# Seven block products for the gate projections of a hybrid encoder block, and half of the merged tensor through DRAM

## The chip, the cores and the metric

The kernel runs on all 8 cores of one Trainium2 chip, one batch element of 2048 tokens on each core, with the same weights everywhere and no exchange between cores. The metric is device time of the slowest core in microseconds, from one execution to the next the median of the runs.

## The reference, cut to what matters

Every token is normalised and goes through one wide input projection. Two branches (a gated convolution, `y_c`, and a diagonal state-space scan, `y_s`) are built from the first 5120 columns; the last 4096 columns are the logits of two sigmoid gates, and the branches meet under these gates:

```python
xn = _rmsnorm(h, norm_g)
proj = jnp.einsum("bld,de->ble", xn, w_in)
v_c, g_c, z_c, u_s, z_s, gl_c, gl_s = _split_columns(proj)
...
gate_c = jax.nn.sigmoid(gl_c + b_gate[:D_MODEL])
gate_s = jax.nn.sigmoid(gl_s + b_gate[D_MODEL:])
merged = (gate_c * jnp.einsum("ble,ed->bld", y_c, w_conv)
          + gate_s * jnp.einsum("ble,ed->bld", y_s, w_ssm))
h = h + jnp.einsum("bld,de->ble", merged, w_out)
out = _rmsnorm(h, final_g)
```

D_MODEL is 2048, `y_c` and `y_s` have 1024 channels each. 16 meta tokens are put in front of the 2048 and dropped at the end. The gate logits are a product of 4096 columns with 2048 inputs for each token, the largest single product of the block.

## The kernel before, in words

Channels lie on the 128 partitions, tokens run along the free dimension. Matmuls take bf16 operands, 128 x 128 weights against 512 tokens, into one of 8 PSUM banks. On-chip memory is cut by hand into regions: XM (the normalised tokens, 16 blocks of 128 channels), CY (working space, later the two branches `CBv` and `YSv`), WS (weights), ST (everything short-lived) and SM (small parameters). Tokens are held in eight chunks `j` of 258 (time modulo 8; two of the 258 belong to the meta tokens), so a block `n` of 512 tokens is two chunks read in two runs of 256; `rt(n)` is that view.

The stages follow one another: normalisation with the first projections, the scan and the convolution, the z projections (written to DRAM in `z_scr` and read back through the slots `zr`), layer norm and the GLU of the scan branch (lines 1096 to 1155), then the stage that the change rewrites (lines 1180 to 1205), then the output projection with its normalisation (lines 1208 to 1349).

The rewritten stage runs over two halves `h` of the tokens and 16 tiles `j` of 128 output channels; the text calls one pair (h, j) a unit. A unit loads three weight tiles through the POOL queue (`gload`, eight rotating slots in WS): the two gates' 2048 x 128 weights and the branch tile, 1024 x 128 for each branch. For each of its two blocks of 512 tokens it runs two gate projections of 16 matmuls, a sigmoid of each on ScalarE (`gst`, fp32), two branch projections of 8 matmuls, a multiply of each with its gate on VectorE (`stt`) and an addition of the two into the merged tensor (`tt`). A unit so has 64 gate and 32 branch matmuls. The merged tensor of half 0 is kept in ST, that of half 1 in XM over the tokens of half 0 (`MGv`).

The output stage then takes 16 blocks of 128 tokens in the order of `blocks`, multiplies each with w_out (64 matmuls, four banks of 512 columns), adds x, which `o_load` fetches on the SP queue, and normalises. w_out replaces the branches in CY and the tokens of half 1 in XM as these are freed.

The order of the instructions is not written by hand. `Sched` (line 73) is a list scheduler that runs while the program is built: each operation carries an engine, an estimated duration, its dependences and a priority (`prio`, lower first); the scheduler steps through a model time, and each free engine takes the ready operation with the lowest priority number, then the earliest in program order. The resulting order of each engine and each DMA queue is fixed, and `resolve` adds semaphore waits for the dependences. A buffer (`Buf`) is an interval of a region, so that reuse of space makes a wait as well. Main matmuls have priority 40 (`P_MAIN`), evictions 3.

Of the kernel before, what the change touches and what calls it, by code (L numbers as in the profile page):

```python
# [22 lines left out]
NC = L // T  # L23
# [322 lines left out]
def build():  # L346
    nc = bass.Bass("TRN2", target_bir_lowering=False)
    Buf.registry = {}
    S = Sched()
# [10 lines left out]
    w_main = din("w_main", [72, 128, 2048])  # L360
    w_br = din("w_br", [16, 128, 2048])
# [5 lines left out]
    def scratch(name, shape):  # L367
        return nc.dram_tensor(name, list(shape), BF16).ap()
# [5 lines left out]
    c_scr = scratch("c_scr", [8, 8, 128, NR])  # L374
    z_scr = scratch("z_scr", [16, 128, SEQ])
    k_scr = scratch("k_scr", [8, 8, 16, 240])

    es = ExitStack()
    with es:
# [25 lines left out]
        def tile(region, lo, nbytes, dt=BF16):  # L405
            return view(region, lo, nbytes, dt), Buf((region, lo, lo + nbytes))


        def act(out_, in_, func, bias=0.0, scale=1.0, accum=None, n=512, reads=(), writes=(), **kw):
            kw["tab"] = {AF.Sqrt: "sqrt", AF.Exp: "exp", AF.Ln: "exp", AF.Sin: "silu", AF.Tanh: "silu", AF.Silu: "silu",  # L410
                         AF.Sigmoid: "sigmoid", AF.Gelu_apprx_tanh: "gelu"}.get(func)
            if accum is None:
                f = lambda e: e.activation(out=out_, in_=in_, func=func, bias=bias, scale=scale)  # L413
            else:
                f = lambda e: e.activation(out=out_, in_=in_, func=func, bias=bias, scale=scale, accum_out=accum)
            return S.op("act", f, 0.22 + n / 1200.0, reads, writes, **kw)

        def tt(out_, in0, in1, op, n=512, rate=0.96, reads=(), writes=(), eng="dve", **kw):
            d = 0.15 + n / (rate * 1000.0) if eng == "dve" else 0.3 + n * 2.2e-3
            return S.op(eng, lambda e: e.tensor_tensor(out=out_, in0=in0, in1=in1, op=op), d, reads, writes, **kw)  # L420
# [628 lines left out]
        def rt(n):  # L1049

            return lambda k: XMv[:, k, 2 * n * NC:(2 * n + 2) * NC].rearrange("p (j c) -> p j c", j=2)[:, :, 2:NC]

        def xrt(n):
            return xb_of(2 * n * NC, (2 * n + 2) * NC)
# [43 lines left out]
        zr = [tile("ST", 36864 + i * 2048, 2048) for i in range(3)]  # L1098
        zr_n = [0]

        zr += [tile("ST", 6144 + i * 2048, 2048) for i in range(8)]

        def z_load(mm, h, prio):
            i = zr_n[0] % 3 if mm > 7 else 3 + mm
            zr_n[0] += 1
            dma("sp", [(zr[i][0], z_scr[mm][:, h * 1024:(h + 1) * 1024])], f"zr{i}", 128 * 2048,
                (zscB[mm][2 * h], zscB[mm][2 * h + 1]), (zr[i][1],), prio=prio)
            return zr[i]
# [30 lines left out]
        for n in range(4):  # L1139
# [11 lines left out]
            if n % 2:  # L1151
# [8 lines left out]
        MGB_ = [[[Buf((("ST", j * 2048 + q * 1024, j * 2048 + q * 1024 + 1024) if h == 0 else  # L1160
                       ("XM", j * L * 2 + q * 1024, j * L * 2 + q * 1024 + 1024))) for q in range(2)] for j in range(16)]
                for h in range(2)]
        gst = [tile("ST", 32768 + i * 2048, 2048, F32) for i in range(4)]
        all_n = [0]

        def any_bank():
            b = all_n[0] % 8
            all_n[0] += 1
            return b

        gn = 0
        g_slot = [0]
        marks = []

        def gload(src_ap):
            s_ = g_slot[0] % 8
            g_slot[0] += 1
            return wload(s_, src_ap, 33, after=(zm,) if 6 <= g_slot[0] <= 8 else ())

        for h in range(2):  # L1180
            for j in range(16):
                gw = [gload(w_main[40 + 2 * j])[:2], gload(w_main[41 + 2 * j])[:2]]
                b3, brB, _ = gload(w_br[j])
                for n in (2 * h, 2 * h + 1):
                    q = n % 2
                    dst = MGv[h][:, j, q * 512:q * 512 + 512]
                    gs = []
                    for br_ in range(2):
                        bk = any_bank()
                        proj(gw[br_][0], gw[br_][1], 0, rt(n), 512, xrt(n), bk)  # L1190
                        g_, gB = gst[gn % 4]
                        gn += 1
                        bc = PAR["bgate"][:, 16 * br_ + j:16 * br_ + j + 1]
                        act(g_, ps[bk], AF.Sigmoid, bias=bc, reads=(psB[bk], psmB), writes=(gB,), prio=3)
                        gs.append((g_, gB))
                    for br_, (sv, sB) in enumerate(((CBv, CBq), (YSv, YSq))):
                        bk = any_bank()
                        proj(b3[:, br_ * 8:br_ * 8 + 8, :], brB, 0, lambda k: sv[:, k, n * 512:(n + 1) * 512], 512,
                             [sB[k][n] for k in range(8)], bk, nk=8, halves=1)
                        g_, gB = gs[br_]  # L1200

                        stt(g_, ps[bk], 1.0 - 0.5 * br_, g_, ALU.mult, ALU.mult, reads=(psB[bk], gB), writes=(gB,), prio=3)
                    mk = tt(dst, gs[0][0], gs[1][0], ALU.add, reads=(gs[0][1], gs[1][1]), writes=(MGB_[h][j][q],), prio=3)
                    if h:
                        marks.append(mk)


        CYk = CY[:, :].rearrange("p (k t) -> p k t", k=16)
# [33 lines left out]
            fst.append((v_, b_))  # L1242
        xp = x.rearrange("(c j) d -> j c d", j=8)
        op_ = out.rearrange("(c j) d -> j c d", j=8)
        blocks = [(j, hf) for j in range(8) for hf in range(2)]

        def o_load(i):
            j, hf = blocks[i]
            v_, b_ = ht[i % 8]
            dma("sp", [(v_, xp[j, 128 * hf:128 * hf + 128, :].rearrange("c (n t) -> c n t", n=4))], f"ht{i % 8}",  # L1250
                128 * 8192, (), (b_,), prio=6)
# [79 lines left out]
        FIRST = 8  # L1331
        for i in range(8):
            o_load(i)
        for i in range(FIRST):
            for n in range(2):
                o_mm(i, n)
# [136 lines left out]
```

How the kernel before makes its waits and increments, by code:

```python
    def emit(self, name, eng):  # L335
        for waits, o, sig in self.prog[name]:
            for sem, v in waits:
                eng.wait_ge(sem, v)
            last = len(o.fns) - 1
            for i, fn in enumerate(o.fns):
                ins = fn(eng)
                if o.dsrc is not None or i == last:
                    ins.then_inc(sig[0], sig[1])
# [1016 lines left out]
                @block.sync  # L1360
                def _(e):
                    S.emit("sp", e)
                    for src, v in last.values():
                        e.wait_ge(src.sem, v)
```

## Time and profile before

| | |
|---|---|
| median of 3 runs | 1683.8 us |
| lowest and highest | 1683.55 and 1696.59 us |
| profiled execution, span of its slowest core | 1678.5 us |
| spans of the 8 cores in it | 1665.3 to 1678.5 us |
| PE, VectorE, ScalarE, POOL busy | 1631.0, 706.7, 554.6, 106.9 us |
| rewritten stage | 784.06 to 1447.10 us of the span |
| output stage | from 1447.10 us |

The span is from the first to the last instruction on a core. The profiled execution has no time of its own on the page beside its span; the runs were timed apart from it, and their times contain what lies around the span. PE is the matrix engine, PEld its weight loads, DVE the VectorE, ACT the ScalarE. Matmuls are pipelined, and their ends are modelled, so that one takes 380 ns in a row although the next starts long before; the distance from start to start is read from counts over a stretch.

### The profile page before, as it was taken

To read this page: it belongs to the slowest core of one execution; us is meant where nothing else is said; L and a number is where in the kernel's file an instruction comes from. 1 tells how busy PE (TensorE), PEld (TensorE's weight loads), DVE (VectorE), ACT (ScalarE), POOL (GpSimd) and SP (SyncE) were. 2 spreads that over 40 slices of the span, in tenths; PEclk is the share of its full clock that TensorE was granted. 3 is DMA by queue.
4 is the path that set the end of the run, shared out by engine and by line. 5 is a ranking of instruction groups with operands and counts; after the bars stand their busy time and mean duration, and the time that the engine had idled before them with its cause. 6 is when DMAs were issued, how large, how long until landed. Compare 5 with 4: busy or idle time off the path is not lost.

```text
span 1678.5 us, 25748 instructions; the slowest of 8 cores (1665.3 to 1678.5 us)
## 1 busy us (share of the span) xinstructions
PE 1631.0 (97%) x9426; PEld 928.3 (55%) x9512; DVE 706.7 (42%) x1262; ACT 554.6 (33%) x954; POOL 106.9 (6%) x206
## 2 busy tenths in 40 slices
PE   7999989998999999999999999999999999999997
PEld 6888868887855444444444444444444444444443
DVE  3799158786777110578111111111111221225433
ACT  4564346454455169554111111111111111122222
POOL 1000000010001000000100000000110100100000
PEclk9999999999999999999999999999999999999999
DMA  9935979889577654443644444445555553837612
GB/s 239 218 90 103 144 95 148 143 142 145 110 153 161 160 148 98 113 108 94 113 76 75 76 76 76 76 76 89 100 93 92 101 93 81 184 98 237 215 76 76
DMA packets 115163, 200.86 MB, mean 120 GB/s; under 512 B 19424, under 2 KB 68832, under 8 KB 112864
## 3 DMA queue, kind: packets, MB, share of 16 engines
q0 software_dynamic: 33792, 92.29, 35.2%
q1 hardware_dynamic: 80672, 105.35, 22.9%
q8 instruction: 78, 1.28, 0.3%
q10 hardware_dynamic: 576, 1.58, 0.3%
q14 instruction: 45, 0.37, 0.1%
HBM read 248.92 MB, written 42.53 MB: 174 GB/s over the span
## 4 chain that ended last, share of the span: by engine, by line
PE 89%; DMA 4%; DVE 2%; SPq 2%; issue 2%; ACT 1%; DVEq 0%; ACTq 0%; POOLq 0%
PE ps L446 88%; DMA WS<-w_dw 2%; SPq L458 2%; DVE CY L420 1%; DMA WS<-w_main 1%; DMA CY<-x_t 1%; DMA CY<-u_scr 1%; ACT CY L413 0%; DVE CY L431 0%; PE ps L737 0%; ACT L413 0%; DVE XM L431 0%; DVE ST L431 0%; PE ps L725 0%; DVE CY L979 0%
## 5 line engine op out<-in xcount | busy, mean ns | idle before, releaser
L446 PE MATMUL ps<-XM,WS 128*128 128x258 bf16 (+1 forms) x6144 | 1044.0, 329 | 5.9 <-DVE XM L431 2.2
L446 PEld LDWEIGHTS ps<-XM,WS 128*128 128x128 bf16 x6144 | 603.1, 98 | 409.5 <-issue 12.9
L413 ACT ACTIVATE ST<-ps,SM 128x512 f32<-128x512 f32 (+2 forms) x224 | 137.2, 626 | 622.8 <-PE ps L446 619.2
L431 DVE SCALAR_TENSOR_TENSOR ST<-ps,ST 128x512 f32<-128x512 f32 x132 | 91.3, 692 | 529.1 <-PE ps L446 529.1
L446 PE MATMUL ps<-CY,WS 128*128 128x512 bf16 x1217 | 282.3, 379 | 3.3
L446 PEld LDWEIGHTS ps<-CY,WS 128*128 128x128 bf16 x1280 | 125.1, 98 | 151.1
L420 DVE TENSOR_TENSOR CY<-CY 128x512 bf16<-128x512 f32 (+4 forms) x184 | 120.9, 658 | 28.0 <-PE ps L446 11.4
L413 ACT ACTIVATE ST<-ps 128x258 f32<-128x258 f32 (+1 forms) x136 | 65.0, 483 | 148.7 <-PE ps L446 145.2
L420 DVE TENSOR_TENSOR CY<-ps,CY 128x514 f32<-128x514 f32 (+2 forms) x97 | 66.1, 683 | 109.7 <-PE ps L446 108.8
L413 ACT ACTIVATE CY<-CY 128x514 f32<-128x514 f32 (+3 forms) x112 | 82.3, 751 | 55.9 <-DVE CY L420 30.4
L458 POOL DMA_DIRECT2D WS<-w_main x104 | 55.2, 531 | 684.9 <-PE ps L446 530.2
L420 DVE TENSOR_TENSOR ST<-ST 128x512 f32<-128x512 f32 (+3 forms) x87 | 56.0, 650 | 68.0 <-ACT ST L1090 47.2
L420 DVE TENSOR_TENSOR CY<-CY,ST 128x512 f32<-128x512 f32 (+3 forms) x115 | 64.3, 594 | 14.0 <-DMA CY<-par_b 7.0
L436 ACT CAST ST<-ps 128x258 bf16<-128x258 f32 (+1 forms) x96 | 41.9, 438 | 64.3 <-PE ps L446 58.5
L446 PE MATMUL ps<-CY 128*128 128x256 bf16 (+1 forms) x320 | 52.6, 279 | 8.6 <-DMA CY<-u_scr 5.7
L431 DVE SCALAR_TENSOR_TENSOR XM<-CY,SM,ST 128x258 bf16<-128x258 f32 x128 | 52.8, 483 | 19.2 <-ACT ST L413 19.2
L446 PE MATMUL ps<-XM 128*128 128x512 bf16 (+1 forms) x267 | 56.3, 367 | 0.3
L446 PE MATMUL ps<-CY,XM 128*128 128x512 bf16 x251 | 56.1, 379 | 0.3
L446 PE MATMUL ps<-CY,ST 128*128 128x512 bf16 x251 | 55.2, 380 | 0.3
L446 PE MATMUL ps<-XM,ST 128*128 128x512 bf16 x251 | 55.2, 380 | 0.3
L413 ACT ACT_TABLE_LOAD x35 | 44.9, 1283 | 27.0 <-PE ps L446 13.5
L446 PE MATMUL ps<-ST,WS 128*128 128x256 bf16 x320 | 41.9, 281 | 10.5 <-DMA WS<-w_dw 8.9
(82 smaller groups left out, 799.4 us busy)
## 6 DMA issues: line engine op xcount, KB each, us to landing
WS<-w_main POOLq DMA_DIRECT2D x104, 512.0 KB, 6.3
WS<-w_br POOLq DMA_DIRECT2D x32, 512.0 KB, 6.2
CY<-x_t SPq DMA_DIRECT2D x30, 516.0 KB, 17.6
WS<-w_dw POOLq DMA_DIRECT2D x32, 320.0 KB, 9.5
z_scr<-ST SPq DMA_DIRECT2D x64, 128.0 KB, 3.1
ST<-z_scr SPq DMA_DIRECT2D x32, 256.0 KB, 3.4
WS<-x SPq DMA_DIRECT2D x8, 1024.0 KB, 8.5
CY<-x SPq DMA_DIRECT2D x8, 1024.0 KB, 12.4
```

What stands on the lines that cost most here:

```text
L413: f = lambda e: e.activation(out=out_, in_=in_, func=func, bias=bias, scale=scale)
L420: return S.op(eng, lambda e: e.tensor_tensor(out=out_, in0=in0, in1=in1, op=op), d, reads, writes, **kw)
L431: return S.op("dve", lambda e: e.scalar_tensor_tensor(out=out_, in0=in0, scalar=scalar, in1=in1, op0=op0, op1=op1), 0.15 + n / 960.0, read ...
L436: return S.op("act", lambda e: e.copy(out=out_, in_=in_), 0.22 + n / 1200.0, reads, writes, **kw)
L446: return lambda e: e.matmul(a[0], a[1], a[2], start=a[3], stop=a[4])
L458: return lambda e: e.dma_start(out=o, in_=i, allow_slow_non_contiguous=True)
```

## The change

In each unit but the first of each half (j = 0), the gate logits of 256 output columns (both gates) and 1024 tokens are computed as a 2 x 2 block product by the Winograd form of Strassen's scheme. Blocks of the weights are gate (conv, ssm) by half of the 2048 inputs, blocks of the tokens are half of the inputs by block of 512 tokens. There are seven products of 8 matmuls each instead of eight. Three sums of the tokens (`T3`, `T2`, `T4`, new tiles in ST) and one in place in XM are made once per half by VectorE (`token_sums`, after the j = 0 unit), four sums of the weights in each unit. Four of the products accumulate in one bank, `ba`; ScalarE copies the bank out between them, and VectorE adds another bank to three of the copies.

ST so has no room for the merged tensor of half 0: each of its pieces goes through a small tile to DRAM (`m_scr`) and comes back into ST on the SP queue before its output blocks. The output stage takes the blocks of half 1 first. The weights go into two fixed sets instead of eight slots, `gst` has seven places instead of four, and `zr` has one place less. The load of w_out and the output stage itself are as before. A cut diff:

```diff
+    m_scr = scratch("m_scr", [16, 128, 1024])
...
-        zr += [tile("ST", 6144 + i * 2048, 2048) for i in range(8)]
+        zr += [tile("ST", 8192 + i * 2048, 2048) for i in range(7)]
 
         def z_load(mm, h, prio):
-            i = zr_n[0] % 3 if mm > 7 else 3 + mm
+            i = zr_n[0] % 3 if mm > 7 else 3 + mm % 7
...
+        mscB = [[Buf() for _ in range(2)] for _ in range(16)]
+        mst = [tile("ST", 38912 + i * 1024, 1024) for i in range(4)]
+        gst = [tile("ST", lo, 2048, F32) for lo in (22528, 24576, 26624, 28672, 16384, 18432, 20480)]
...
+        T3, T2, T4 = [view("ST", lo, 8192).rearrange("p (k t) -> p k t", k=8) for lo in (30720, 0, 8192)]
+        TB = [[Buf(("ST", lo + i * 4096, lo + i * 4096 + 4096)) for i in range(2)] for lo in (30720, 0, 8192)]
...
+        def token_sums(h):
+            n0, n1 = 2 * h, 2 * h + 1
+            t4 = lambda t, i: t[:, 4 * i:4 * i + 4, :].rearrange("p k (j c) -> p k j c", j=2)
+            kw = dict(n=2048, rate=1.92, prio=4.5)
+            for i in range(2):
+                (b11, r11), (b12, r12), (b21, r21), (b22, r22) = xq(n0, i), xq(n1, i), xq(n0, 2 + i), xq(n1, 2 + i)
+                tt(t4(T3, i), b22, b12, ALU.subtract, reads=r22 + r12, writes=(TB[0][i],), **kw)
+            for i in range(2):
+                (b11, r11), (b12, r12), (b21, r21), (b22, r22) = xq(n0, i), xq(n1, i), xq(n0, 2 + i), xq(n1, 2 + i)
+                tt(t4(T2, i), t4(T3, i), b11, ALU.add, reads=r11 + [TB[0][i]], writes=(TB[1][i],), **kw)
+            for i in range(2):
+                (b11, r11), (b12, r12), (b21, r21), (b22, r22) = xq(n0, i), xq(n1, i), xq(n0, 2 + i), xq(n1, 2 + i)
+                tt(b12, b12, b11, ALU.subtract, reads=r11 + r12, writes=r12, **kw)
+            for i in range(2):
+                (b11, r11), (b12, r12), (b21, r21), (b22, r22) = xq(n0, i), xq(n1, i), xq(n0, 2 + i), xq(n1, 2 + i)
+                tt(t4(T4, i), b21, t4(T2, i), ALU.subtract, reads=r21 + [TB[1][i]], writes=(TB[2][i],), **kw)
...
+        def product(bk, wv, wB, rhs, rB, first):
+            def mk(k):
+                return lambda e: e.matmul(ps[bk], wv[:, k, :], rhs(k), start=first and k == 0, stop=k == 7, skip_group_check=True)
+            return S.op("pe", [mk(k) for k in range(8)], 8 * 0.2157, [wB] + rB, (psB[bk],), prio=P_MAIN)
...
+        def merge(h, j, q, g0, g1):
+            (a, aB), (b, bB) = g0, g1
+            if h:
+                marks.append(tt(MGv[1][:, j, q * 512:q * 512 + 512], a, b, ALU.add, reads=(aB, bB), writes=(MGB_[1][j][q],), prio=3))
+                return
+            mt, mB = mst[(2 * j + q) % 4]
+            tt(mt, a, b, ALU.add, reads=(aB, bB), writes=(mB,), prio=3)
+            dma("sp", [(m_scr[j][:, q * 512:q * 512 + 512], mt)], f"ms{(2 * j + q) % 4}", 128 * 1024, (mB,), (mscB[j][q],), prio=5,
+                store=True)
...
-                gw = [gload(w_main[40 + 2 * j])[:2], gload(w_main[41 + 2 * j])[:2]]
-                b3, brB, _ = gload(w_br[j])
...
-                        proj(gw[br_][0], gw[br_][1], 0, rt(n), 512, xrt(n), bk)
...
+                t_ = 16 * h + j
+                (wc, ws_, b3), (wcB, wsB, brB), ((wc0B, wc1B), (ws0B, ws1B)), (s1, s2), (s1B, s2B) = gset[t_ % 2]
+                for e, src in ((0, w_main[40 + 2 * j]), (1, w_main[41 + 2 * j]), (2, w_br[j])):
+                    dma("pool", [((wc, ws_, b3)[e], src.rearrange("p (k n) -> p k n", k=16))], f"g{t_ % 2}{e}", 128 * 2048 * 4, (),
+                        ((wcB, wsB, brB)[e],), prio=33)
+                if j == 0:
+                    for q in range(2):
...
+                    token_sums(h)
+                    continue
+                kw = dict(n=1024, rate=1.92, prio=8)
+                a11, a12, a21, a22 = wc[:, 0:8, :], wc[:, 8:16, :], ws_[:, 0:8, :], ws_[:, 8:16, :]
+                tt(s1, a21, a22, ALU.add, reads=(ws0B, ws1B), writes=(s1B,), **kw)
+                tt(s2, s1, a11, ALU.subtract, reads=(s1B, wc0B), writes=(s2B,), **kw)
+                tt(a21, a11, a21, ALU.subtract, reads=(wc0B, ws0B), writes=(ws0B,), **kw)
+                ba, bb, bc = any_bank(), any_bank(), any_bank()
+                rq = lambda n, kh: [XB[jj][q] for jj in (2 * n, 2 * n + 1) for q in (2 * kh, 2 * kh + 1)]
+                xk = lambda n, kh: (lambda k: rt(n)(8 * kh + k))
+                tk = lambda t: (lambda k: t[:, k, :])
+                gc0, gc1, gs0, gs1 = gslot(), gslot(), gslot(), gslot()
+                product(ba, a11, wc0B, xk(n0, 0), rq(n0, 0), True)
+                cp("act", gc0[0], ps[ba], reads=(psB[ba],), writes=(gc0[1],), prio=2.5)
+                product(bb, a12, wc1B, xk(n0, 1), rq(n0, 1), True)
+                tt(a12, a12, s2, ALU.subtract, reads=(s2B, wc1B), writes=(wc1B,), **kw)
+                tt(gc0[0], ps[bb], gc0[0], ALU.add, reads=(psB[bb], gc0[1]), writes=(gc0[1],), prio=3)
+                gate(gc0, gc0[0], gc0[1], 0, j)
+                product(ba, s2, s2B, tk(T2), TB[1], False)
+                cp("act", gc1[0], ps[ba], reads=(psB[ba],), writes=(gc1[1],), prio=2.5)
+                product(bc, s1, s1B, xk(n1, 0), rq(n1, 0), True)
+                product(ba, a21, ws0B, tk(T3), TB[0], False)
+                cp("act", gs1[0], ps[ba], reads=(psB[ba],), writes=(gs1[1],), prio=2.5)
+                tt(gs1[0], ps[bc], gs1[0], ALU.add, reads=(psB[bc], gs1[1]), writes=(gs1[1],), prio=3)
+                gate(gs1, gs1[0], gs1[1], 1, j)
+                branch(h, j, 0, 0, gc0, b3, brB)
+                product(ba, a22, ws1B, tk(T4), TB[2], False)
+                gate(gs0, ps[ba], psB[ba], 1, j)
+                branch(h, j, 1, 1, gs1, b3, brB)
+                product(bc, a12, wc1B, xk(n1, 1), rq(n1, 1), False)
+                tt(gc1[0], ps[bc], gc1[0], ALU.add, reads=(psB[bc], gc1[1]), writes=(gc1[1],), prio=3)
+                gate(gc1, gc1[0], gc1[1], 0, j)
+                branch(h, j, 0, 1, gs0, b3, brB)
+                merge(h, j, 0, gc0, gs0)
+                branch(h, j, 1, 0, gc1, b3, brB)
+                merge(h, j, 1, gc1, gs1)
...
-        blocks = [(j, hf) for j in range(8) for hf in range(2)]
+        blocks = [(j % 8, hf) for j in range(4, 12) for hf in range(2)]
...
+        for q in range(4):
+            dma("sp", [(MG0[:, 4 * q:4 * q + 4, :], m_scr[4 * q:4 * q + 4].rearrange("k p t -> p k t"))], f"mg{q}", 128 * 8192,
+                [b for k in range(4 * q, 4 * q + 4) for b in mscB[k]], [b for k in range(4 * q, 4 * q + 4) for b in MGB_[0][k]],
+                prio=7, packets=512)
```

`branch` is the old branch projection with its multiply, `gate` the old sigmoid, `gslot` the next place of `gst`, `xq` the view of four channel blocks of one block of tokens, `gset` the two weight sets.

## Rows read from the trace of the kernel before

**Rows 1.** The page: busy time per engine, and the chain that ended last.

```profile
PE 1631.0 (97%) x9426; PEld 928.3 (55%) x9512; DVE 706.7 (42%) x1262; ACT 554.6 (33%) x954; POOL 106.9 (6%) x206
...
PE 89%; DMA 4%; DVE 2%; SPq 2%; issue 2%; ACT 1%; DVEq 0%; ACTq 0%; POOLq 0%
```

**Rows 2.** Windows: stretch, length, busy by engine (instructions), clock, DMA share, GB/s.

```profile
784.06:1447.10 663.04, 660.06 (x3017) 300.28 (x3073) 141.73 (x207) 89.92 (x130) 60.02 (x107) 1.00 0.49 86
...
300.00:400.00 100.00, 92.89 (x827) 79.75 (x825) 75.79 (x153) 50.72 (x104) 9.63 (x18) 0.96 0.91 140
...
500.00:600.00 100.00, 97.95 (x501) 49.52 (x501) 42.24 (x78) 41.31 (x74) 6.44 (x12) 0.97 0.68 160
...
700.00:800.00 100.00, 99.64 (x458) 45.25 (x463) 70.12 (x112) 45.16 (x65) 4.14 (x8) 1.00 0.40 106
```

**Rows 3.** Groups, 784 to 1447: shape, count, busy us, mean ns, idle before.

```profile
L446 PEld LDWEIGHTS ps<-XM,WS 128*128 128x128 bf16 x2048 | 200.2, 98 | 241.8
L446 PEld LDWEIGHTS ps<-CY,WS 128*128 128x128 bf16 x1024 | 100.1, 98 | 120.9
L413 ACT ACTIVATE ST<-ps,SM 128x512 f32<-128x512 f32 x128 | 88.0, 687 | 567.5 <-PE ps L446 567.5
L431 DVE SCALAR_TENSOR_TENSOR ST<-ps,ST 128x512 f32<-128x512 f32 x127 | 87.8, 692 | 514.2 <-PE ps L446 514.2
```

**Rows 4.** The chain in order of time: start, length, one link of this stretch.

```profile
980.47 10.74 PE ps L446 x49
```

**Rows 5.** Groups, 784 to 805: the z multiplies at the end of the GLU.

```profile
L420 DVE TENSOR_TENSOR CY<-CY,ST 128x1024 bf16<-128x1024 bf16 x9 | 5.8, 684 | 2.5 <-DMA ST<-z_scr 2.5
```

**Rows 6.** Timeline, three places: start, length, instruction, idle time before it.

```profile
744.77 39.66 PE L446 MATMUL ps<-CY,WS 128*128 128x512 bf16 x179
744.88 0.69 ACT L413 ACTIVATE ST<-ps,SM 128x512 bf16<-128x512 f32 x1 [0.40 <-PE ps L446]
...
780.00 0.80 ACT L413 ACTIVATE ST<-ST,SM 128x512 f32<-128x512 f32 x1
780.90 0.69 DVE L420 TENSOR_TENSOR CY<-ST 128x512 bf16<-128x512 f32 x1 [2.10 <-ACT ST L413]
...
1514.14 2.35 DVE L431 SCALAR_TENSOR_TENSOR WS<-WS,SM,ST 128x2048 f32<-128x2048 f32 x1 [0.18 <-DVE SM L440]
```

**Rows 7.** Windows around the start of the stretch (third busy column is VectorE).

```profile
780.00:790.00 10.00, 9.95 (x47) 4.55 (x47) 6.56 (x11) 4.82 (x7) 0.00 (x0) 1.00 0.20 60
790.00:800.00 10.00, 9.95 (x47) 4.49 (x46) 6.43 (x11) 1.38 (x3) 2.03 (x4) 1.00 0.01 2
800.00:810.00 10.00, 9.95 (x47) 4.54 (x47) 2.08 (x3) 1.37 (x2) 1.14 (x3) 1.00 0.99 152
```

**Rows 8.** The page: DMA issues, count, KB each, median us to landing.

```profile
WS<-w_br POOLq DMA_DIRECT2D x32, 512.0 KB, 6.2
...
ST<-z_scr SPq DMA_DIRECT2D x32, 256.0 KB, 3.4
```

**Rows 9.** Tiles: SP's last z loads and first x loads, with their starts.

```profile
L458 SPq DMA_DIRECT2D ST<-z_scr x26: 319/320/322, 703.6 to 784.9; - x26
...
L458 SPq DMA_DIRECT2D WS<-x x8: 328/340/457, 1406.1 to 1543.4; - x8
```

**Rows 10.** Windows after the stretch; the last two columns are DMA share, GB/s.

```profile
1440.00:1450.00 10.00, 9.95 (x47) 4.57 (x47) 2.08 (x3) 1.37 (x2) 2.96 (x4) 1.00 1.08 203
...
1470.00:1480.00 10.00, 9.95 (x47) 4.56 (x47) 2.08 (x3) 1.93 (x5) 0.00 (x0) 1.00 1.11 271
1480.00:1490.00 10.00, 9.95 (x47) 4.50 (x47) 2.08 (x3) 1.81 (x7) 0.00 (x0) 1.00 0.32 107
1490.00:1500.00 10.00, 10.00 (x48) 4.52 (x47) 1.93 (x3) 2.04 (x6) 0.00 (x0) 1.00 0.00 0
1500.00:1510.00 10.00, 9.95 (x47) 4.57 (x47) 1.71 (x4) 2.17 (x6) 0.00 (x0) 1.00 0.01 2
```

More of the change, by code:

```diff
@@ L1162, in build @@
                 for h in range(2)]
-        gst = [tile("ST", 32768 + i * 2048, 2048, F32) for i in range(4)]
+        mscB = [[Buf() for _ in range(2)] for _ in range(16)]
+        mst = [tile("ST", 38912 + i * 1024, 1024) for i in range(4)]
+        gst = [tile("ST", lo, 2048, F32) for lo in (22528, 24576, 26624, 28672, 16384, 18432, 20480)]
         all_n = [0]
@@ L1169, in any_bank, with gslot @@
             return b
-        gn = 0
-        g_slot = [0]
-        marks = []
[L1175 to L1178, printed above, removed]
+        gst_n = [0]
+        def gslot():
+            gst_n[0] += 1
+            return gst[(gst_n[0] - 1) % 7]
+        T3, T2, T4 = [view("ST", lo, 8192).rearrange("p (k t) -> p k t", k=8) for lo in (30720, 0, 8192)]
+        TB = [[Buf(("ST", lo + i * 4096, lo + i * 4096 + 4096)) for i in range(2)] for lo in (30720, 0, 8192)]
@@ new lines, in xq @@
+        def xq(n, q):
+            v = XMv[:, 4 * q:4 * q + 4, 2 * n * NC:(2 * n + 2) * NC].rearrange("p k (j c) -> p k j c", j=2)[:, :, :, 2:NC]
+            return v, [XB[2 * n][q], XB[2 * n + 1][q]]
+        def token_sums(h):
[14 more added lines that the diff above has]
+                tt(t4(T4, i), b21, t4(T2, i), ALU.subtract, reads=r21 + [TB[1][i]], writes=(TB[2][i],), **kw)
@@ new lines, in build @@
+        marks = []
+        gset = []
+        for i in range(2):
+            lo = 16384 * i
+            w = [tile("WS", lo + 4096 * e, 4096) for e in range(3)]
+            v = [t.rearrange("p (k n) -> p k n", k=16) for t, _ in w]
+            hb = [[Buf(("WS", lo + 4096 * e + 2048 * u_, lo + 4096 * e + 2048 * u_ + 2048)) for u_ in range(2)] for e in range(2)]
+            sums = [tile("WS", lo + 12288 + 2048 * e, 2048) for e in range(2)]
+            gset.append((v, [b for _, b in w], hb, [t.rearrange("p (k n) -> p k n", k=8) for t, _ in sums], [b for _, b in sums]))
@@ new lines, in branch, with gate @@
+        def branch(h, j, q, br_, g, b3, brB):
+            n = 2 * h + q
+            sv, sB = ((CBv, CBq), (YSv, YSq))[br_]
+            bk = any_bank()
+            proj(b3[:, br_ * 8:br_ * 8 + 8, :], brB, 0, lambda k: sv[:, k, n * 512:(n + 1) * 512], 512,
+                 [sB[k][n] for k in range(8)], bk, nk=8, halves=1)
+            stt(g[0], ps[bk], 1.0 - 0.5 * br_, g[0], ALU.mult, ALU.mult, reads=(psB[bk], g[1]), writes=(g[1],), prio=3)
+        def gate(g, src, sB, br_, j):
+            act(g[0], src, AF.Sigmoid, bias=PAR["bgate"][:, 16 * br_ + j:16 * br_ + j + 1], reads=(sB, psmB), writes=(g[1],), prio=3)
@@ L1180, in build @@
         for h in range(2):
+            n0, n1 = 2 * h, 2 * h + 1
             for j in range(16):
-                gw = [gload(w_main[40 + 2 * j])[:2], gload(w_main[41 + 2 * j])[:2]]
-                b3, brB, _ = gload(w_br[j])
[L1184 to L1189, printed above, removed]
-                        proj(gw[br_][0], gw[br_][1], 0, rt(n), 512, xrt(n), bk)
[L1191 to L1205, printed above, removed]
@@ new lines, in build @@
+                t_ = 16 * h + j
[5 more added lines that the diff above has]
+                    for q in range(2):
+                        n = 2 * h + q
+                        gs = []
+                        for br_, (wv, wB) in enumerate(((wc, wcB), (ws_, wsB))):
+                            bk = any_bank()
+                            proj(wv, wB, 0, rt(n), 512, xrt(n), bk)
+                            g = gslot()
+                            gate(g, ps[bk], psB[bk], br_, j)
+                            gs.append(g)
+                        for br_ in range(2):
+                            branch(h, j, q, br_, gs[br_], b3, brB)
+                        merge(h, j, q, *gs)
+                    token_sums(h)
+                    continue
```

## The prediction

> **What bounds the kernel now.** I read four views in order. First the page: PE is busy 97% of the span and no other engine half of it [rows 1]. A busy PE need not be at its peak, so I next asked for PE by stretch. The stretch the change rewrites, from the first gate projection to the last branch projection, is 663.04 us long; PE is busy 660.06 us of it at a granted clock of 1.00 (the 2.4 GHz level), with VectorE at 141.73 us, ScalarE at 89.92 and the DMA share at 0.49 [rows 2]. Third, the groups of that stretch: 2048 weight loads for gates and 1024 for branches, one per matmul (some matmul records are missing, so I count the loads) [rows 3]. 663.04 / 3072 = 0.2158 us per matmul of 512 columns: a stream without gaps, in which a matmul taken out is worth its 0.2158 us. Last, the chain of waits is PE for 89% [rows 1], and in this stretch it is PE only, in links like the one in [rows 4]. So the stretch ends when PE has issued everything; ScalarE and VectorE wait for PE, not the other way round [rows 3].
>
> **The change, part by part.**
>
> *Fewer matmuls.* A unit (one half of the tokens, one tile of output channels) has 64 gate and 32 branch matmuls. With seven products of 8 matmuls the gates need 56. Units with j = 0 keep the old form, so 30 of 32 units save 8: 240 x 0.2158 = **51.8 us off**, all on the path. A unit goes from 20.7 to 19.0 us, the stretch from 663.0 to 611.2.
>
> *VectorE inside a unit.* Added: four weight sums of 1024 bf16 elements and three additions out of PSUM. The nearest row to a weight sum is the z multiply, same size, type and instruction: 684 ns; an addition out of PSUM is 692 like the branch multiply [rows 5, 3]. Added 4 x 0.684 + 3 x 0.692 = 4.8 us; with the four multiplies and two merges that stay (4.1 us) VectorE has 8.9 us of work in 19.0. ScalarE gets three copies on top of four sigmoids: 7 x 0.687 = 4.8 us. Both lie beside PE, priced at nothing; if the cover went, 4.8 us a unit.
>
> *A new wait of PE.* Four products accumulate one after the other in one bank, `ba`, and ScalarE copies the bank out after each of the first three. The next product into `ba` waits for that copy, and behind it on PE's in-order queue waits all the rest. No row shows such a hand-off, so I build it from neighbours. In the earlier GLU stage, also groups of 8 matmuls, ScalarE starts reading a bank 0.11 us after the next group has begun (PE 744.77, ScalarE 744.88) and needs 0.69 [rows 6]. ScalarE to another engine takes 0.10 us (end 780.80, VectorE start 780.90) [rows 6]. So a copy is known 0.11 + 0.69 + 0.10 = 0.90 us into the covering group, which lasts 8 x 0.2158 = 1.73. Each pair of `ba` products has exactly one other group of 8 between; slack 0.83 us. The tightest is the copy behind the sigmoid of `gc0`, which waits for VectorE's addition: addition over at 0.80, sigmoid from 0.90 to 1.59, copy due at 1.84. It is late for PE only if that addition is held up by 0.25 + 0.83 = 1.1 us, one and a half VectorE instructions. Lower bound 0; upper bound with every copy uncovered 3 x 0.90 x 30 = 81 us. I take **+1 us**, nearer to 0, because the cover is there in program order.
>
> *Token sums, twice.* After each j = 0 unit VectorE makes eight sums of 2048 bf16 elements in runs of 256. No row has this shape. Bounds: two z multiplies, 1.37 us, or the fp32 instruction of 2048 elements, 2.35 us [rows 5, 6], so 10.9 to 18.8 us a set. At the first set VectorE is busy 6.56, 6.43 and 2.08 us in the three 10 us slices from 780 [rows 7]: about 15 us idle, plus 3.5 us of unit 1 whose first two products need no sums. At 1.37 us the set and unit 1's first weight sums (2.1 us) fit; at 2.35 us they overrun by 18.8 + 2.1 - 18.5 = 2.4, and the in-place sums, which must wait for the last gate projection of the j = 0 unit, push it to some 10. The second set meets a VectorE with only 2.08 us per 10 [rows 7] and costs nothing. I take 1.37, the row of the same type, and **+1.5 us** for the join, range 0 to 10. The Trainium skill, page "VectorE: DVE Perf Modes", section "What auto-detection actually checks", says a `tensor_tensor` runs two elements a cycle when every tensor is 16-bit with step 1, whatever the outer strides; its table has 1224 ns for 2048 bf16. By it the sum would be 1 us lower. The z multiply agrees (684 ns, against 692 for half as many fp32); the strided shape no run here shows.
>
> *Queues.* POOL: the same 96 weight loads, now in two sets instead of eight slots. A set's last load starts when unit t is over and lands 6.2 us later [rows 8]; unit t+2 starts 19 us later. Nothing. SP: 32 stores of the merged half, 128 KB each; SP has nothing between the last z load at 784.9 and the first x load at 1406.1 [rows 9]. Nothing. One z slot less delays the eighth z multiply by a load (3.4 us [rows 8]) on VectorE, which is not waited for until the branches. Nothing; without that cover, 3.4 us.
>
> *The change of stage.* Output blocks now start with the half just merged, and the other half (4.2 MB) comes back from DRAM. Its last tile is needed by the second half of a 16-matmul group, 1.73 us after the stretch ends, against two VectorE instructions, 1.4 us: nothing, else about 1 us once. The four reloads share the DMA engines with x and w_out. Now these run full for four slices, 1440 to 1480, at 203 to 271 GB/s, then 0.32 of a slice, and stand idle until 1510, while w_out's second half is first wanted after 8 blocks of two banks, 256 x 0.2158 = 55 us after the stretch, at 1502 [rows 10]. Two reloads can go early, as their space is free 7 to 13 us before the end; all four at 250 GB/s are 17 us against about 19 idle. The first eight blocks take 8 x 64 x 0.2158 = 110 us, so the reload itself is hidden. Price 0, bounds 0 to 8 us (half the transfer on the path). SP holds x loads behind a reload that waits; eight banks of 3.45 us stand before PE feels that. Nothing here can gain either: PE has no gap to give back.
>
> **Sum.** Profiled execution: 1678.5 - 51.8 + 1 + 1.5 = 1629.2 us of span. The page gives no time for it beyond the span; the median of the runs lies 1683.8 - 1678.5 = 5.3 us above. So **1634 us**, ratio 0.971.
>
> **Rivals.**
> - *Sums at one element a cycle, or w_out late* (10%): the upper ends of the two terms above, 8 to 16 us, so 1642 to 1650. For: no row of the strided shape; the DMA margin is a few us. Against: the z multiply row.
> - *The clock slips* (5%). VectorE goes from 21 to 47% and ScalarE from 14 to 25%. Between 500 and 600, with 42 and 41%, the granted clock was 0.97; between 700 and 800, with 70 and 45%, it was 1.00 [rows 2]. At 0.97 the 611 us grow by 19: 1653. The Trainium skill, "TensorE: Matmul & The Clock Gate", section "A second HAM failure mode: psum-queue depth-cycling", describes micro-idles between groups that cycle through PSUM banks as enough to make the clock go back and forth; here it would act at the `ba` hand-offs. Rows 2 speak against it: groups through eight banks at 1.00 for 663 us.
> - *The hand-offs eat the gain* (4%). The stretch then looks like 300 to 400, where PE, fed by the other two engines, is busy 92.89% [rows 2]: 611 / 0.93 = 657, so 1680. Against: 0.83 us of slack.
> - *Slower* (4%): ScalarE is in order, and if the copy of `ba` stands behind a sigmoid whose addition stands behind weight sums, all three copies of a unit are uncovered: 81 us, 1634 - 1 + 81 = 1714. It decides from 51.8 / 30 = 1.73 us lost per unit. VectorE would have to be a full three instructions behind in every unit; at 47% load I see nothing that makes it so.
> - *The change does not do what it says* (1%): with 64 gate matmuls a unit still there, 1684. The loop has seven calls of eight, taken by 30 units, so this is read off, not guessed.
>
> **How the numbers follow.** Forecast 76%, own range 1630 to 1640. To leave out 2 in 10 at most I let in the first rival's upper end: 1629 to 1650; below, 1683.8 - 51.8 = 1632 with both added terms at zero, less 3 for the median's own spread. A difference of 1% (17 us) is about what a measurement of this kernel can tell from none. Faster by over 1% means under 1667: the forecast and the first two rivals, 0.91. Within 1%: the third and the last, 0.05. Slower by over 1%: 0.04.
>
> **What would show it.** The rewritten stretch should be about 612 us with 2832 weight loads, a granted clock of 1.00 and PE waiting on ScalarE for less than 0.1 us a unit. Token sums show as eight VectorE instructions of 2048 elements: 1.2 to 1.4 us right, above 2 wrong. A PE gap at the second unit shows the join; a gap 55 us after the stretch, released by w_out, shows the DMA term. The output stage should keep its 221 us. I am wrong if the time saved per unit is clearly less than 1.73 us, and the releaser in that gap says which term it was.

## The result, and the profile after

The changed kernel takes **1636.7 us** (median of 5 runs) against 1687.2 for the kernel before, timed beside it: ratio 0.970, 95% interval 0.967 to 0.973. In each set of five one execution was far longer (1759.1 and 1920.5 us); the ratio and its interval are of the others. The forecast was 1634, range 1629 to 1650. The profiled execution took 1635.4 us, with a span of 1633.5 on its slowest core.

The page of the changed kernel, busy time per engine and the chain that ended last, as in [rows 1]:

```profile
PE 1579.0 (97%) x9272; PEld 902.1 (55%) x9272; DVE 856.3 (52%) x1488; ACT 606.5 (37%) x1044; POOL 107.0 (7%) x206
...
PE 84%; DMA 6%; DVE 4%; issue 2%; SPq 2%; ACT 1%; DVEq 0%; ACTq 0%; POOLq 0%
```

PE is as full as before, with 52 us less work; VectorE has 150 us more of it. 9512 weight loads before, 9272 now: the 240 are gone.

Two windows of the same kernel, the rewritten stretch (first gate weight load to first weight load of the output stage) and the output stage. Columns as in [rows 2]:

```profile
787.03:1401.38 614.35, 612.01 (x2833) 276.62 (x2832) 289.44 (x431) 142.74 (x220) 59.48 (x106) 1.00 0.60 101
1401.38:1633.50 232.12, 221.43 (x1042) 101.76 (x1040) 90.97 (x139) 52.27 (x149) 0.00 (x0) 0.99 0.55 167
```

On this core the stretch went from 663.04 to 614.35 us, still at a granted clock of 1.00, with VectorE busy 47% of it (289.44 us, from 141.73 in [rows 2]) and ScalarE 23%. Over the eight cores it is 612.01 to 614.35, median 612.44; before, 663.04 on all of them. So **the stretch gives 50.6 us**; the medians of the runs differ by 50.5.

From here on I compare the lengths of this stretch and of the output stage, median of the cores, not whole times. PE's instructions ahead of the stretch are in the same order in both kernels, but the time at which a core gets there differs by some 10 us from one execution to the next, more than several of the effects sought.

The groups of the stretch, which answer to [rows 3], with the three new ones:

```profile
L447 PEld LDWEIGHTS ps<-CY,WS 128*128 128x128 bf16 x1024 | 100.2, 98 | 120.8
L1217 PEld LDWEIGHTS ps<-XM,WS 128*128 128x128 bf16 x960 | 93.9, 98 | 113.3
L1217 PEld LDWEIGHTS ps<-ST,WS 128*128 128x128 bf16 x720 | 69.9, 98 | 88.6 <-issue 5.4
...
L432 DVE SCALAR_TENSOR_TENSOR ST<-ps,ST 128x512 f32<-128x512 f32 x127 | 87.6, 690 | 133.5 <-PE ps L447 133.5
L421 DVE TENSOR_TENSOR WS<-WS 128x1024 bf16<-128x1024 bf16 x120 | 79.8, 686 | 31.3 <-DMA WS<-w_main 30.2 <-DVE WS L421 1.1
L437 ACT COPY ST<-ps 128x512 f32<-128x512 f32 x90 | 52.2, 580 | 187.6 <-PE ps L1217 187.2
```

30 units x 56 = 1680 loads for products (960 with tokens as they are, 720 with sums of tokens). A weight sum takes 686 ns (684 forecast), a copy 580 (687 forecast). VectorE's wait for the branches' PSUM is down to 133.5 us from 514.2. It is still idle for half of the stretch, but now in other places too: 30.2 us of it are waits for weights, in its weight sums. That new wait returns below.

Where PE waits in the changed kernel. Columns: who waits <- for what: total us, times, longest. From 787 to the end:

```profile
PE ps L1217 <- ACT ST L437: 2.3, 4, 1.0
...
DVE WS L421 <- DMA WS<-w_main: 30.2, 28, 2.6
...
DVE WS L421 <- DMA WS<-x: 23.3, 2, 16.1
```

Of 90 hand-offs from ScalarE's copy to PE, 4 show a wait, 2.3 us together on this core, the one with the most; the others have 0.4 to 2.0 us.

### The profile page after: what moved, and what is told of

Its sections match the earlier page's. It is cut to its first block, busy times and chain, and to the rows that moved or that the text cites. A ratio compares the mean times of both kernels' runs of the same rounds, so it can differ in the third digit from the quotient of the medians.

```text
span 1633.5 us, 25838 instructions; the slowest of 8 cores (1616.0 to 1633.5 us)
## 1 busy us (share of the span) xinstructions
PE 1579.0 (97%) x9272; PEld 902.1 (55%) x9272; DVE 856.3 (52%) x1488; ACT 606.5 (37%) x1044; POOL 107.0 (7%) x206
## 4 chain that ended last, share of the span: by engine, by line
PE 84%; DMA 6%; DVE 4%; issue 2%; SPq 2%; ACT 1%; DVEq 0%; ACTq 0%; POOLq 0%
PE ps L447 62%; PE ps L1217 21%; DMA WS<-w_dw 3%; DMA WS<-w_main 2%; DVE CY L421 2%; SPq L459 2%; DMA CY<-u_scr 1%; DMA CY<-x_t 1%; ACT CY L414 1%; DVE CY L980 0%; DVE CY L432 0%; PE ps L738 0%; ACT ST L414 0%; ACT L414 0%; DVE ST L432 0%
## 5 line engine op out<-in xcount | busy, mean ns | idle before, releaser
L447 PE MATMUL ps<-XM,WS 128*128 128x258 bf16 (+1 forms) x4224 | 615.6, 304 | 5.7 <-DVE XM L432 2.7
L447 PEld LDWEIGHTS ps<-XM,WS 128*128 128x128 bf16 x4224 | 414.4, 98 | 179.4 <-issue 7.0
L1217 PE MATMUL ps<-XM,WS 128*128 128x512 bf16 x960 | 221.9, 379 | 0.0
L414 ACT ACTIVATE ST<-ST,SM 128x512 f32<-128x512 f32 (+1 forms) x123 | 91.7, 748 | 229.0 <-DVE ST L421 228.5
L1217 PE MATMUL ps<-ST,WS 128*128 128x512 bf16 x720 | 170.1, 379 | 2.3 <-ACT ST L437 2.3
L1217 PEld LDWEIGHTS ps<-XM,WS 128*128 128x128 bf16 x960 | 93.9, 98 | 113.3
L421 DVE TENSOR_TENSOR ST<-ps,ST 128x512 f32<-128x512 f32 x90 | 62.0, 689 | 143.1 <-ACT ST L437 111.1
L437 ACT COPY ST<-ps 128x512 f32<-128x512 f32 x90 | 52.2, 580 | 187.6 <-PE ps L1217 187.2
L414 ACT ACTIVATE ST<-ps,SM 128x256 bf16<-128x256 f32 (+2 forms) x134 | 75.2, 584 | 121.4 <-PE ps L447 72.6
L1217 PEld LDWEIGHTS ps<-ST,WS 128*128 128x128 bf16 x720 | 69.9, 98 | 88.6 <-issue 5.4
L421 DVE TENSOR_TENSOR WS<-WS 128x1024 bf16<-128x1024 bf16 x120 | 79.8, 686 | 31.3 <-DMA WS<-w_main 30.2
```

Of the source, the lines that this page charges most:

```text
L437: return S.op("act", lambda e: e.copy(out=out_, in_=in_), 0.22 + n / 1200.0, reads, writes, **kw)
L447: return lambda e: e.matmul(a[0], a[1], a[2], start=a[3], stop=a[4])
L1217: return lambda e: e.matmul(ps[bk], wv[:, k, :], rhs(k), start=first and k == 0, stop=k == 7, skip_group_check=True)
```

## Experiments

All are edits of the changed kernel. My theory: the stretch is PE's stream at 0.2158 us a matmul, and the added work is hidden as long as each copy fits into its covering group. The rivals: the time comes from the new output order, or from a cheaper matmul; a hidden cost in the hand-offs, the join or the reloads has eaten part of the gain. The output stage is counted to the last instruction; the 221 us that the prediction gives it are PE's part, from its first weight load to the end of its last matmul (221.43 us before and after). The last column is against the kernel before, timed beside each.

| kernel | stretch us | output us | whole time against before |
|---|---|---|---|
| before | 663.04 | 231.44 | 1 |
| changed | 612.44 | 232.09 | 0.970 [0.967, 0.973] |
| e1_old_products | 663.04 | 232.09 | 1.000 [0.996, 1.005] |
| e2_first_half | 637.14 | 232.09 | 0.982 [0.972, 0.991] |
| e3_copy2 | 621.53 | 232.08 | 0.975 [0.966, 0.985] |
| e4_copy4 | 726.43 | 232.10 | 1.036 [1.025, 1.047] |
| e5_sums_twice | 620.68 | 232.43 | one execution |
| e6_extra_dma | 612.87 | 232.31 | one execution |
| e7_late_sums | 611.24 | 232.16 | 0.970 [0.967, 0.973] |
| e8_early_dma | 614.83 | 246.41 | one execution |
| e9_early_dma2 | 613.10 | 271.56 | one execution |

**The matmuls, e1 and e2.** Eight products in every unit, everything else of the change kept; then the seven products in half 0 alone.

```diff
# e1
-                if j == 0:
+                if True:
...
-                    token_sums(h)
# e2
-                if j == 0:
+                if j == 0 or h:
...
-                    token_sums(h)
+                    if h == 0:
+                        token_sums(h)
```

> All that the change rearranges (DRAM pass of half the merged tensor, order of the output blocks, two weight sets, gst and zr slots) with the old gate projections in all 32 units and no token sums: the seven-product units are left out. If PE alone sets the end and the rest is hidden, the rewritten stage takes 663 us as before, the output stage 232, and the ratio to the kernel before is 1.00. If the rearrangement gives or takes a part of the 50 us, the ratio differs from 1.00 by that part, in the stage where it acts.

> Seven products only in the 15 units of the first half of the tokens, old gates in the second. If the gain is 0.2158 us for each matmul left out, 120 matmuls give 25.9 us: stage 637 to 638 us, time about 1661, ratio 0.985. If the gain came from one place (the joins, the output stage, the transfers), it would not be halved: 1637 or 1685.

e1's stretch is 663.04 us on every core, that of before to the last digit; e2's is 637.14 in the median, that is 25.9 less, or 120 x 0.2158. A window inside e1's stretch shows a PE without a gap:

```profile
780.00:1425.00 645.00, 645.00 (x2990) 292.42 (x2989) 131.35 (x191) 85.40 (x124) 56.52 (x102) 1.00 0.55 97
```

So the whole gain is the matmuls taken out, linear in their number. The road through DRAM, the two weight sets and the turned block order give and cost nothing in the stretch, and nothing in PE's part of the output stage. The 0.65 us by which that stage is longer (232.09 against 231.44, in e1 too) lie behind the last matmul: at the end of the program SP waits for every DMA semaphore in turn, 115 before and 128 now. Line, queue, instruction, count, shortest, median and longest in ns, first and last start; before, then changed:

```profile
L1364 SPq EVENT_SEMAPHORE  x115: 17/17/17, 1672.2 to 1678.2; - x115
```

```profile
L1460 SPq EVENT_SEMAPHORE  x128: 17/17/17, 1626.5 to 1633.2; - x128
```

The waits follow each other at about 0.05 us (6.0 us for 114 steps, 6.7 for 127), and 13 more are 0.65 us.

**The hand-offs, e3 and e4.** After each copy of `ba`, one or three copies more of the same bank into the same place.

```diff
                 cp("act", gc0[0], ps[ba], reads=(psB[ba],), writes=(gc0[1],), prio=2.5)
+                for _ in range(3):        # e3: 1
+                    S.op("act", lambda e, o=gc0[0], p=ps[ba]: e.copy(out=o, in_=p), 0.001, (psB[ba],), (gc0[1],), prio=2.4)
# the same behind the copies into gc1 and gs1
```

> Each copy out of the shared bank is made twice in a row, in otherwise unchanged order. With 0.59 us a copy, 0.11 to begin and 0.10 to report, the second ends 1.4 us into a covering group of 1.73: by the slack theory PE loses 0 to 10 us in the whole stage (the copy behind the sigmoid is the tight one). If the copies already stood at the limit, 0.59 x 90 = 53 us would be lost, and the time would be that of the kernel before.

> The same with four copies in a row: 0.11 + 4 x 0.59 + 0.10 = 2.6 us against a cover of 1.73, so 0.85 us late at each of 90 hand-offs. By the slack theory the stage grows by some 75 us (60 to 95), the kernel is slower than before (about 1710), and PE's waits name ScalarE's copies. If PE does not in fact hang on the copies, nothing changes (1637).

A hand-off of e4 on the timeline. Columns: start, length, engine, line, operation and tiles; in brackets the wait ahead of it and what ended it.

```profile
1012.90 1.89 PE L1217 MATMUL ps<-XM,WS 128*128 128x512 bf16 x8
1013.15 0.59 ACT L437 COPY ST<-ps 128x512 f32<-128x512 f32 x1 [0.51 <-PE ps L1217]
1013.83 1.93 ACT L1285 COPY ST<-ps 128x512 f32<-128x512 f32 x3
...
1015.90 1.89 PE L1217 MATMUL ps<-ST,WS 128*128 128x512 bf16 x8 [1.11 <-ACT ST L1285]
```

Read it from the start of the covering group: the copy begins 0.25 us in and takes 0.59; 0.09 later the three others begin and take 1.93; 0.14 after them PE goes on. That is 3.00 us against the 1.73 in which PE issues the group: 1.27 late, times 90 is 114 us. The stretch grew by 726.43 - 612.44 = 114.0. I had expected less for e4 (60 to 95), since I had taken less for what lies between the instructions. With one copy more, 0.25 + 0.59 + 0.09 + 0.64 + 0.14 = 1.71: just covered, and the 9.1 us of e3 are the hand-offs that something else makes late, now without slack to absorb it: on its profiled core PE's only waits for copies (7, 6.1 us together) are for the one into `gc1`, behind the sigmoid.

The waits of PE in e4, one row for each of the three hand-offs of a unit, and its stretch:

```profile
PE ps L1217 <- ACT ST L1277: 33.7, 30, 1.3
PE ps L1217 <- ACT ST L1290: 33.4, 30, 1.1
PE ps L1217 <- ACT ST L1285: 33.4, 30, 1.1
```

```profile
771.35:1497.00 725.65, 625.89 (x2834) 270.69 (x2832) 292.18 (x435) 305.52 (x492) 59.06 (x106) 1.00 0.49 86
```

All 90 are listed, 100.5 us; the other 14 are PE's busy time grown from 612.01 to 625.89, since the last matmul before a stop counts with its whole modelled length. So **the slower rival is real as a mechanism**: with uncovered copies the change loses 3.6%, on the other side of its break-even of 1.73 us a unit. It did not happen in the changed kernel because 0.98 us of hand-off stands in 1.73 of cover.

**What makes four copies late, e7.** On the timeline of the changed kernel a late hand-off looks so:

```profile
1329.20 1.29 DVE L421 TENSOR_TENSOR WS<-WS 128x1024 bf16<-128x1024 bf16 x2 [2.65 <-DMA WS<-w_main]
...
1329.63 1.89 PE L1217 MATMUL ps<-XM,WS 128*128 128x512 bf16 x8
1330.41 0.69 DVE L421 TENSOR_TENSOR ST<-ps,ST 128x512 f32<-128x512 f32 x1
...
1331.19 0.72 ACT L414 ACTIVATE ST<-ST,SM 128x512 f32<-128x512 f32 x1 [4.17 <-DVE ST L421]
1331.82 0.57 ACT L437 COPY ST<-ps 128x512 f32<-128x512 f32 x1
...
1332.53 1.89 PE L1217 MATMUL ps<-ST,WS 128*128 128x512 bf16 x8 [1.01 <-ACT ST L437]
...
1334.26 1.89 PE L447 MATMUL ps<-CY,WS 128*128 128x512 bf16 x8
1334.51 0.59 ACT L437 COPY ST<-ps 128x512 f32<-128x512 f32 x1 [2.12 <-PE ps L1217]
```

From the top: a weight sum of a later unit stands at the head of VectorE's queue and waits 2.65 us for its weights; behind it stand the addition out of PSUM, then on ScalarE the sigmoid of `gc0`, then the copy, which starts 2.19 us into its covering group (1329.63), and last PE, 1.01 us late. The other three late ones on this core look the same, with 1.82 to 2.18 us of waiting for weights. The last two lines are the next hand-off, in time: copy 0.25 us into its group. In e7 the planner takes the weight sums' data to be there 5 us later than before, and so puts them further back in VectorE's queue; PE's order is the same.

```diff
-                kw = dict(n=1024, rate=1.92, prio=8)
+                kw = dict(n=1024, rate=1.92, prio=8, margin=5.0)
```

> The planner is told that weights come 5 us later, so that VectorE's sums of the next unit's weights stand later in its order; nothing else moves. If PE's few waits on the copies come from an addition held up behind a weight sum that waits for its weights, these waits (2.3 us now) fall under 0.5 and the stage goes from 612 to 614 to about 611.5. If they come from the hand-off itself, they stay. The time changes by less than a measurement can tell.

The same place in e7 (its slowest core): the addition first, the weight sum after it.

```profile
1336.90 0.69 DVE L421 TENSOR_TENSOR ST<-ps,ST 128x512 f32<-128x512 f32 x1 [1.96 <-PE ps L1217]
1337.51 0.68 DVE L421 TENSOR_TENSOR WS<-WS 128x1024 bf16<-128x1024 bf16 x1
1337.68 0.72 ACT L414 ACTIVATE ST<-ST,SM 128x512 f32<-128x512 f32 x1 [2.01 <-DVE ST L421]
...
1338.29 1.89 PE L1217 MATMUL ps<-XM,WS 128*128 128x512 bf16 x8
1338.54 0.59 ACT L437 COPY ST<-ps 128x512 f32<-128x512 f32 x1
```

The copy again starts 0.25 us into its group. VectorE's wait for weights, 30.2 us on 28 occasions in the changed kernel, is in e7:

```profile
DVE WS L421 <- DMA WS<-w_main: 1.0, 2, 0.7
```

PE waits for no copy any more, and the stretch is 611.24 us on all eight cores; 2832 x 0.2158 = 611.15. That is PE's floor for this count of matmuls. The 1.2 us against the median core of the changed kernel (3.1 against its slowest) can't be told apart in whole times (0.970 both).

**The join behind the token sums, e5.** Each of the three sums into new tiles is made a second time.

```diff
                 tt(t4(T3, i), b22, b12, ALU.subtract, reads=r22 + r12, writes=(TB[0][i],), **kw)
+                S.op("dve", lambda e, o=t4(T3, i), a=b22, b=b12: e.tensor_tensor(out=o, in0=a, in1=b, op=ALU.subtract), 0.001, r22 + r12, (TB[0][i],), prio=4.4)
# the same for T2 and T4
```

> Six of the eight token sums of each half are made twice (the two in place are not), with PE's order unchanged: 6 x 1.17 = 7 us more for VectorE at each join. If the first join is as full as the sum said, PE stops 4 to 7 us at the first product that needs a sum, and the stage takes 617 to 620 us; at the second join, where VectorE is freer, nothing. If VectorE has room at the first join too, the stage stays at 612 to 614.

First the token sums of the changed kernel, whose first gate weight load is at 787.03:

```profile
784.66 2.36 DVE L421 TENSOR_TENSOR ST<-XM 128x2048 bf16<-128x2048 bf16 x2
...
801.23 1.22 DVE L421 TENSOR_TENSOR ST<-ST,XM 128x2048 bf16<-128x2048 bf16 x1
...
803.50 2.35 DVE L421 TENSOR_TENSOR XM<-XM 128x2048 bf16<-128x2048 bf16 x2
...
811.38 1.43 PEld L1217 LDWEIGHTS ps<-ST,WS 128*128 128x128 bf16 x8 [0.29 <-issue]
```

One sum takes 1.22 us (a pair 2.35). The load for the first product made of sums alone, `s2` with `T2`, has 0.29 us of idle time ahead of it, and its matmuls still follow the group before without a gap. In e5 they wait, and the row of the window behind shows a lower clock:

```profile
810.19 3.35 PE L1220 MATMUL ps<-ST,WS 128*128 128x512 bf16 x8 [5.69 <-DVE WS L421]
```

```profile
810.00:813.00 3.00, 2.81 (x7) 1.04 (x8) 2.83 (x6) 0.72 (x1) 0.00 (x0) 0.50 0.00 0
```

Of the set's 6 x 1.22 = 7.3 us more, 5.7 reach PE at once, on every core. Then the granted clock is 0.50 (the 1.2 GHz level), and on this core the next group begins 3.19 us after this one, not 1.73: 1.5 us more. The stretch is 8.2 longer in the median; at the second join PE shows no wait. So the join was full: it cost next to nothing, but had next to no margin either. Sums at one element a cycle, the first rival, add 8 x (2.35 - 1.22) = 9.0 us a set and would, as an estimate from e5, have cost about that much.

**The reloads, e6, e8, e9.** Copies of the merged half from DRAM to DRAM, as many transfers again (e6, e8: 4.2 MB; e9: 8.4 MB), on the SP queue beside the reloads. The results are written to a buffer that nobody reads.

```diff
+        for q in range(4):        # e9: 8
+            dma("sp", [(m2_scr[4 * q:4 * q + 4], m_scr[4 * q:4 * q + 4])], f"mx{q}", 128 * 64,
+                [b for k in range(4 * q, 4 * q + 4) for b in mscB[k]], (), prio=7, after=(marks[-1],))
# e8, e9: prio=5.5, after=(marks[-3],); e9's second four read and write as the first, into a second buffer
```

> Behind the four reloads SP issues four more transfers of 1 MB, DRAM to DRAM, that nobody needs: 4.2 MB, 17 us of the DMA engines at 250 GB/s, in the crowded stretch after the rewritten stage. If the margin there is the few us that the DMA row leaves (w_out's last part lands some 9 us before its use), PE stops 0 to 8 us where w_out's second half begins, or at the first x tile that comes late. If the transfers are hidden with room to spare, the output stage stays at 232 us.

> The four extra transfers of 1 MB, DRAM to DRAM, now stand on SP some 18 us before the end of the rewritten stage, ahead of the reloads and most x loads, so that they and w_out compete. If the margin is the 7.6 us that w_out's last part now has, 4.2 MB at 250 GB/s (17 us), less what finds the engines idle before the crowd, make PE stop 0 to 8 us in the output stage. If nothing there hangs on transfers, the stage stays at 232.1 us.

> The same with eight transfers, 8.4 MB, 34 us of the engines. If the margin is a few us, PE must now stop 10 to 25 us in the output stage, released by a transfer of w_out or x. If PE still does not stop, the transfers of the change of stage have far more room than the sum gave them.

e6 missed its aim. Its transfers were issued at 1450.4 to 1457.0, behind the reloads and w_out, whose last part had been issued at 1407.0 and landed at about 1459.5. The output stage stayed at 232.3 (0.2 more are four semaphores more at the end), which says nothing of the margin. e8 and e9 put them ahead; the waits, first of e8, then of e9:

```profile
PE ps L448 <- DVE WS L422: 11.0, 1, 11.0
PE ps L448 <- DMA XM<-w_out: 4.2, 1, 4.2
...
DVE WS L422 <- DMA WS<-x: 41.7, 2, 25.9
```

```profile
PE ps L448 <- DVE WS L422: 36.8, 2, 28.3
```

The output stage grew by 14.3 us (e8) and 39.5 (e9), more than the expectations had: PE's first wait is for VectorE's addition of x, which waits for an x tile behind the crowded transfers; w_out is the second. In the changed kernel w_out's last part was issued at 1399.6 and landed 52.8 us later (the `max` below), at 1452.4; 280 matmuls of the output stage come ahead of its first use (where e8's second wait is), so that is at 1401.38 + 280 x 0.2158 = 1461.8: 9 us of margin. The first wait of e8 is ahead of matmul 225, which needs the bank of the seventh group; in the changed kernel that matmul is due at 1401.38 + 224 x 0.2158 = 1449.7, and the addition that frees the bank ended at 1442.8: 7 us. Columns of the first line: shortest, median, longest; the windows as in [rows 10]:

```profile
DMA to landing us min/median/max: 7.4/10.1/52.8
```

```profile
1440.00:1450.00 10.00, 10.00 (x48) 4.52 (x47) 2.77 (x4) 2.21 (x7) 0.00 (x0) 1.00 0.90 247
1450.00:1460.00 10.00, 10.00 (x48) 4.55 (x47) 3.96 (x6) 4.23 (x13) 0.00 (x0) 1.00 0.35 128
```

The last reload landed at 1457.8, and PE has no gap. The 4.2 MB of reloads found free transfer time; the next 4.2 MB did not all find it.

## Why the prediction was right

- **Fewer matmuls**, -51.8 us: as forecast. e7's 611.24 us are 51.8 below 663.04, and e2 gives half.
- **Work beside PE** at nothing: right. VectorE's 289 us and ScalarE's 143 lie under PE.
- **The hand-offs**, +1 us: the stretch is 1.2 us above its floor on the median core and 3.1 on the slowest, with 2.3 of waits for copies there. The parts were off, and cancelled: the copy starts 0.25 us into the group, not 0.11 (a misreading of [rows 6]: PE's 744.77 is where that view's window cuts the stream, at the second matmul of a group that began at 744.56, 0.32 us ahead of ScalarE), takes 0.59, not 0.69, and PE follows after 0.14, not 0.10; 0.98 us for my 0.90, slack 0.75 for 0.83. The tightest place was the one I named, the copy behind the sigmoid that waits for an addition. What holds that addition up I had as one and a half busy VectorE instructions; it is a weight sum that waits for its DMA at the head of the queue. I had priced the weight sums' time and not their wait, although the rival "slower" has the addition stand behind weight sums.
- **The join**, +1.5 us: at most 0.1 (e7 reaches its floor with the join in it). With 1.37 us a sum instead of 1.22 a set would have been 1.2 us longer, and e5 suggests that most of it would have reached PE. The Trainium skill, page "VectorE: DVE Perf Modes", section "The perf-mode tier table (the rule you actually need)", has 1224 ns for a bf16 `tensor_tensor` of 2048 elements; the measurement agrees, with runs of 256 too. That the strided sum might take 2.35 us was the open end, and e5 suggests that it would have been felt.
- **The change of stage**, 0: right for PE, whose part of the output stage is as long as before. The 0.65 us are closing waits, a term that I did not have. The margin I had as "a few us" is about 9 at w_out and 7 at the x tiles; it is these, which I had covered with eight banks, that break first in e8 and e9.
- **The clock**: 1.00 over the stretch, so that rival did not occur. The Trainium skill, page "TensorE: Matmul & The Clock Gate", section "A second HAM failure mode: psum-queue depth-cycling", has micro-idles between groups that cycle through banks make the clock go back and forth; in e4 PE stopped 90 times for about 1.1 us, and the granted clock was 1.00. No run here shows such a swing from many short stops; the clock fell after single longer ones, in e5 and e9.
- **The total**, 2.7 us under the median. The span was 1633.5 for my 1629.2: 3.0 of the difference is the stretch before (787.03 for 784.06, same PE order), 0.6 the rewritten stretch on that core, 0.7 the closing waits. What I added from span to median, 5.3 us, was too much (the profiled execution has 1635.4 - 1633.5 = 1.9), and the two nearly cancel. Since the moment at which a core reaches the stretch differs by some 10 us between executions, so close a total is in part luck. The stretch is not: 613.7 forecast (611.2 and the two terms), 612.44 measured.

## What to carry to other kernels

Where PE ran without a gap at its full granted clock, a matmul taken out was worth exactly its issue time. Whether a scheme that trades matmuls for vector work pays is decided by each hand-off: add up start, copy and return, and compare with what covers it (here 0.98 in 1.73 us). Price an added instruction's wait, not only its time: at the head of an in-order queue it delays whatever stands behind, through as many engines as the chain has. Test a margin by doubling what is to fit; the join and the reloads both looked free, and had no room to be made twice.

## What was not expected of the hardware

In single executions two neighbouring cores run at a lower granted clock in the mixed stage while the others don't, and reach the rewritten stretch some 20 to 30 us later. In e7, from 300 to 400, core 0 and then core 4:

```profile
300.00:400.00 100.00, 95.40 (x751) 78.49 (x750) 68.50 (x135) 45.60 (x96) 9.00 (x17) 0.84 0.75 118
```

```profile
300.00:400.00 100.00, 98.61 (x910) 86.08 (x909) 80.13 (x159) 53.96 (x112) 10.16 (x19) 1.00 0.83 144
```

PE is nearly as busy in both, but core 0 gets through 751 matmuls instead of 910. Between 820 and 1380, inside the rewritten stretch, both have 1.00. What decides which cores are so treated these runs don't show.

A stop of PE can cost more than its length, as at e5's join. In e9, PE stands still from 1440 to 1460 at a granted clock of 0.50 (the 1.2 GHz level), and after the stops the rows read 0.78, 0.73 and 0.93 until 1490, when it is back at 1.00. e4's stops of 1.1 us did nothing of the kind:

```profile
1440.00:1450.00 10.00, 0.00 (x0) 0.00 (x0) 0.00 (x0) 0.00 (x0) 0.00 (x0) 0.50 1.06 249
1450.00:1460.00 10.00, 0.00 (x0) 0.00 (x0) 0.00 (x0) 0.00 (x0) 0.00 (x0) 0.50 1.08 263
1460.00:1470.00 10.00, 8.61 (x32) 3.42 (x32) 1.38 (x2) 1.45 (x4) 0.00 (x0) 0.78 1.09 240
1470.00:1480.00 10.00, 1.70 (x5) 0.62 (x6) 1.38 (x2) 0.87 (x3) 0.00 (x0) 0.73 1.04 275
1480.00:1490.00 10.00, 10.00 (x45) 4.40 (x44) 2.09 (x4) 2.75 (x8) 0.00 (x0) 0.93 0.79 219
```

The second 4.2 MB of copies cost 25.2 us (39.5 - 14.3), while at the 247 GB/s of the window around 1440 they would take 17. That the copies have both ends in DRAM may be part of it; no run tells.

The end of a program has a price for each DMA semaphore. In the changed kernel the last output transfer landed 3.8 us before the last instruction; what is left is SP's 128 waits, 6.7 us from the first to the last, where nearly all semaphores had long been reached. Fewer semaphores to wait for at the end were not tried.
